# The second norm of a two-block transformer kernel, taken by halves of the tokens

## What is computed

```
x  = x + gate1 * einsum('bsm,md->bsd', mixed, w_out)          # output projection
h2 = rms_norm(x, g_norm2) * (1 + scale2) + shift2             # the second norm
q  = einsum('bsd,dq->bsq', h2, w_q_peer)                      # 2048 query columns
scores = einsum('bshpc,hpnc->bshpn', q, sub_keys)             # then top-k, gather, experts
```

## Time and profile before

| | |
|---|---|
| median of three executions | 3136.06 us (3135.14 to 3137.2) |
| span of the profiled execution, first to last instruction | 3134.2 us |
| PE busy, share of the span | 2990.2 us, 95% |
| DVE busy | 2025.2 us, 65% |
| ACT busy | 1261.6 us, 40% |
| POOL busy | 1157.7 us, 37% |

### The profile page before, as it was taken

How to read it: one execution, slowest core, us unless ns; L and a number is a source line. 1 busy time by engine, 2 the same in 40 slices (tenths; PEclk the granted TensorE clock), 3 DMA queues, 4 the chain that set the end, 5 groups by cost and what they waited for, 6 DMA issues and landing times.

```text
span 3134.2 us, 47541 instructions
## 1 busy us (share of the span) xinstructions
PE 2990.2 (95%) x17673; PEld 2612.4 (83%) x17673; DVE 2025.2 (65%) x3238; ACT 1261.6 (40%) x2075; POOL 1157.7 (37%) x564
## 2 busy tenths in 40 slices
PE   6999999998999999999999999899999998999998
PEld 3766679998988888888887788699999975799986
DVE  4767515999977778788886255466651375466622
ACT  3347333446963333333333334432222446432221
POOL 2420333664014444455553222044444430244442
PEclk9998999999999999999999999799999999999999
DMA  6710223555679999999996211023223420122231
GB/s 247 280 60 1 62 93 96 166 175 191 227 248 350 346 328 341 337 351 350 346 347 229 75 55 41 14 88 94 87 88 101 117 81 1 41 89 93 94 101 67
DMA packets 179876, 509.22 MB, mean 162 GB/s; under 512 B 14881, under 2 KB 72353, under 8 KB 175393
## 3 DMA queue, kind: packets, MB, share of 16 engines
q1 hardware_dynamic: 72288, 262.57, 25.4%
q0 software_dynamic: 37440, 136.40, 11.9%
q10 hardware_dynamic: 70016, 108.54, 10.3%
HBM read 467.60 MB, written 39.85 MB: 162 GB/s over the span
## 4 chain that ended last, share of the span: by engine, by line
PE 87%; ACT 5%; DVE 4%; issue 2%; DMA 1%; ACTq 0%; DVEq 0%
PE ps L1279 23%; PE ps L1230 17%; PE ps L1167 16%; PE ps L1533 8%; PE ps L901 8%; ACT arena L1960 2%; PE ps L1351 2%; PE ps L952 1%; ACT arena L1976 1%; PE ps L1680 1%; PE ps L1299 1%; PE ps L1457 1%; PE ps L1414 1%; PE ps L654 1%; PE ps L1421 1%
## 5 line engine op out<-in xcount | busy, mean ns | idle before, releaser
L2314 POOL TENSOR_TENSOR w_lo<-ring,w_hi 128x1024 fp32r<-128x1024 f32 x300 | 755.0, 2520 | 1387.9 <-ACT w_hi L795 1387.8
L795 ACT ACTIVATE w_hi<-ring 128x1024 fp32r<-128x1024 f32 x500 | 525.4, 1055 | 771.9 <-PE ps L1230 277.4
L1230 PE MATMUL ps<-w_hi,arena_r 128*128 128x512 f32 x1536 | 426.8, 397 | 4.5 <-DVE arena_r L2772 4.5
L1167 PE MATMUL ps<-h_hi,w_hi 128*128 128x384 f32 x1024 | 355.5, 347 | 5.0 <-issue 5.0
L1230 PEld LDWEIGHTS ps<-w_hi,arena_r 128*128 128x128 f32 x1536 | 289.0, 189 | 72.2 <-DVE arena_r L2772 5.0
L1167 PE MATMUL ps<-h_lo,w_hi 128*128 128x384 f32 x1024 | 348.9, 341 | 0.0
L1279 PE MATMUL ps<-h_hi,w_hi 128*128 128x264 f32 (+2 forms) x1536 | 347.5, 298 | 0.6 <-DVE arena L2869 0.5
L1167 PE MATMUL ps<-h_hi,w_lo 128*128 128x384 f32 x1024 | 346.4, 338 | 0.0
L1279 PE MATMUL ps<-h_lo,w_hi 128*128 128x264 f32 (+2 forms) x1536 | 346.2, 297 | 0.0
L1279 PE MATMUL ps<-h_hi,w_lo 128*128 128x264 f32 (+2 forms) x1536 | 345.6, 297 | 0.0
L2327 POOL DMA_INDIRECT arena<-u_rows,arena x128 | 193.4, 1511 | 375.8 <-DVE arena L2748 354.5
(11 more groups left out here) (343 smaller groups left out, 5444.0 us busy)
## 6 DMA issues: line engine op xcount, KB each, us to landing
ring<-weight_stream SPq DMA_DIRECT2D x500, 512.0 KB, 3.7
gates<-arena ACTq DMA_DIRECT2D x12, 2048.0 KB, 7.3
arena<-gates ACTq DMA_DIRECT2D x32, 768.0 KB, 14.3
arena<-w_modulation ACTq DMA_DIRECT2D x17, 1024.0 KB, 5.3
early_acts<-arena ACTq DMA_DIRECT2D x64, 192.0 KB, 2.7
arena<-early_acts ACTq DMA_DIRECT2D x32, 384.0 KB, 7.7
arena<-w_modulation ACTq DMA_DIRECT2D x2, 2560.0 KB, 15.0
x<-x_t ACTq DMA_DIRECT2D x1, 2112.0 KB, 19.5
```

Of the source, the lines that this page charges most:

```text
L795: act.activation(w_hi[:, s, :], ring[:, s, :], ACT.Copy).then_inc(hi_ready, 1)
L1167: last = pe.matmul(ps[:, bank, 0:ND], w, v, start=c == 0 and p == 0, stop=c == DC - 1 and p == 2)
L1230: last = pe.matmul(ps[:, Y_BANKS[b][half], :], a[u], w[v][:, half * BANK:(half + 1) * BANK], start=first and p == 0, stop=final and p == 2)
L2314: pool.tensor_tensor(w_lo[:, s, :], ring[:, s, :], w_hi[:, s, :], ALU.subtract)\
```

## The change

The 512 tokens are taken as two halves of 256 from output tile 4 on.

- PE makes output tiles 0 to 3 whole as before. Then it makes tiles 4 to 7 for the first half of the tokens, and after that the same four for the second half, with the same weights in the four slots. The same holds for the first four query tiles. A half tile is 24 matmuls of 256 columns, so the eight halved tiles have 384 matmuls in place of 192.
- The sums of squares are kept by half, the first half's in bank 4, the second's in bank 5. Squares and sums count 12: chunks 0 to 3 whole (two matmuls of 256 columns), chunks 4 to 7 once for each half. The last two sums of the first half stand inside tile 4 of the second half; the last four of the second half stand inside query tile 0 of the first half.
- ACT takes a root for each half and makes 16 high parts of 256 columns in place of 8 of 512. The transfer of the expert keys, which ACT starts, stands behind the first root. The weight splits for the four query slots stand among the high parts of the first half, since those slots are now free only when output tile 4, 5, 6 or 7 is whole.
- DVE adds tiles 4 to 7 by halves and makes the scaled and the low parts by halves, with the adds of the second half among the splits of the first.
- PE starts the first half of query tile 0 only when all eight chunks of that half are split, no longer chunk by chunk.
- The semaphore for the rows of h is one with that of the scores; nothing is moved by that. One more norm group also shifts which of two buffers some later norms use.

The core of the diff (`half_of` and `half_tokens` are the columns of a half):

```diff
+        Norm.squares += halved
+        Norm.sums += halved
+        Norm.groups += 1 if halved else 0
+        Norm.uses += 1 if halved else 0
...
+        Split.chunks += 2 * chunks if halved else chunks
...
+        n_in2 = Norm([every], SEQ, halved=DC // 2)
...
-            for t in range(2, DC):
+            def square_sum(k):
+                c = k if k < DC else k - DC // 2
+                pe.wait_ge(sq_ready, n_in2.q0 + k + 1)
+                for half in (0, 1) if k < DC // 2 else (k // DC,):
+                    cols = half_of(half)
+                    last = pe.matmul(ps[:, 4 + half, cols], ones, sq1[:, (n_in2.q0 + k) % 2, cols],
+                                     start=c == 0, stop=c == DC - 1)
+                last.then_inc(sq_summed, 1)
+            def half_tile(s, half, between=None):
+                for c in range(DC):
+                    h = h_hi[:, c, half_tokens(half)], h_lo[:, c, half_tokens(half)]
+                    for p, (w, v) in enumerate(three(h, weights(s, c * P, (c + 1) * P))):
+                        last = pe.matmul(ps[:, s, half_of(half)], w, v, start=c == 0 and p == 0, stop=c == DC - 1 and p == 2)
+                    if between is not None:
+                        between(c)
+                return last
+            wait(pe, ln_done, n_in2.g0 - 1)
+            for t in range(2, RING):
                 wait(pe, out_added, t - 3)
-                tile1("w_out", TURN["w_out"] + t // 4, t % 4, t % 4)
-                norm_sums(pe, n_in2, ones, [t - 2])
-            norm_sums(pe, n_in2, ones, [6, 7])
-            pe.wait_ge(out_added, DC)
+                tile1("w_out", TURN["w_out"], t, t)
+                square_sum(t - 2)
+            for half in range(2):
+                for s in range(RING):
+                    if half == 0:
+                        pe.wait_ge(out_added, s + 1)
+                        split_wait(pe, "w_out", TURN["w_out"] + 1, s)
+                        half_tile(s, 0).then_inc(half_made, 1)
+                        square_sum(2 + s)
+                    else:
+                        half_tile(s, 1, lambda c: square_sum(6 + (c == 5)) if s == 0 and c in (3, 5) else None) \
+                            .then_inc(slot_used, 1)
+            for half in range(2):
+                for s in range(RING):
+                    if half == 0:
+                        split_wait(pe, "peer_q", TURN["peer_q"], s)
+                    if s == 0:
+                        pe.wait_ge(out_added, DC + half * RING)
+                        pe.wait_ge(h_split, s_in2.q0 + (half + 1) * DC)
+                    last = half_tile(s, half, lambda c: square_sum(DC + c // 2) if half == 0 and s == 0 and c in (0, 2, 4, 6) else None)
+                    if half:
+                        last.then_inc(slot_used, 1)
             def q_tiles(i):
                 if isinstance(i, int):
-                    first_tiles("peer_q", s_in2, part1)
-                for s in range(2 if isinstance(i, int) else 0, RING):
+                    return
+                for s in range(RING):
                     wait(pe, q_peer_taken, i * RING + (s - 3))
                     tile1("peer_q", TURN["peer_q"] + i, s, s)
             turns(pe, 4, q_tiles)
...
-            def split_and_square(name, n, src, ready):
-                for t in range(DC):
-                    split_next(act, name, t // 4, t % 4)
-                    if t:
-                        norm_square(act, n, src, t - 1, ready)
-                norm_square(act, n, src, DC - 1, ready)
-            split_and_square("w_out", n_in2, lambda c: xf[:, c, :], lambda c: act.wait_ge(out_added, c + 1))
+            def square2(k):
+                c = k if k < DC else k - DC // 2
+                cols = slice(0, SEQ) if k < DC // 2 else half_of(k // DC)
+                wait(act, sq_summed, n_in2.s0 + k - 1)
+                act.wait_ge(out_added, k + 1)
+                act.activation(sq1[:, (n_in2.q0 + k) % 2, cols], xf[:, c, cols], ACT.Square).then_inc(sq_ready, 1)
+            def root2(half):
+                act.wait_ge(sq_summed, n_in2.s0 + DC + RING * half)
+                r = rstd1[:, n_in2.g0 % 2, half_of(half)]
+                act.activation(r, ps[:, 4 + half, half_of(half)], ACT.Ln, bias=col("eps", 0), scale=1.0 / D)\
+                    .then_inc(ln_done, 1)
+                act.wait_ge(ln_done, n_in2.g0 + half + 1)
+                act.activation(r, r, ACT.Exp, scale=-0.5).then_inc(rstd_ready, 1)
+            def high2(half, c):
+                if c < DC - 1:
+                    act.wait_ge(h_raw, s_in2.r0 + half * (DC - 1) + c + 1)
+                else:
+                    act.wait_ge(normed, n_in2.u0 + half + 1)
+                act.activation(h_hi[:, c, half_tokens(half)], h_tmp[:, c % 2, half_of(half)], ACT.Identity,
+                               bias=mod[:, 3 * DC + c:3 * DC + c + 1]).then_inc(h_hi_ready, 1)
+            for t in range(RING):
+                split_next(act, "w_out", 0, t)
+                if t:
+                    square2(t - 1)
+            for k in range(RING - 1, DC):
+                square2(k)
+            root2(0)
             act.dma_start(keys, keys_d).then_inc(later_in, 16)
-            norm_root(act, n_in2, 0, 1.0 / D, 0)
+            for s, chunks in enumerate(((0, 1), (2, 3, 4), (5, 6, 7), ())):
+                split_next(act, "w_out", 1, s)
+                if s == 3:
+                    square2(DC + 2)
+                    square2(DC + 3)
+                for c in chunks:
+                    high2(0, c)
+                if s < 2:
+                    square2(DC + s)
+            root2(1)
             for c in range(DC):
-                high_normed(act, s_in2, c, lambda c: mod[:, 3 * DC + c:3 * DC + c + 1])
+                high2(1, c)
...
-            for t in range(DC):
+            def add_out(t, cols):
+                dve.scalar_tensor_tensor(xf[:, t, cols], ps[:, t % 4, cols], mod[:, 2 * DC + t:2 * DC + t + 1],
+                                         xf[:, t, cols], ALU.mult, ALU.add).then_inc(out_added, 1)
+            def add_second(s):
+                dve.wait_ge(slot_used, used(TURN["w_out"] + 1, s))
+                add_out(RING + s, half_of(1))
+            def scaled2(half, c):
+                if c >= 2:
+                    dve.wait_ge(h_split, s_in2.q0 + half * DC + c - 1)
+                dve.scalar_tensor_tensor(h_tmp[:, c % 2, half_of(half)], xf[:, c, half_of(half)], gains[:, 1, c:c + 1],
+                                         rstd1[:, n_in2.g0 % 2, half_of(half)], ALU.mult, ALU.mult)\
+                    .then_inc(*((h_raw, 1) if c < DC - 1 else (normed, 1)))
+            def low2(half, c):
+                dve.wait_ge(h_hi_ready, s_in2.q0 + half * DC + c + 1)
+                dve.scalar_tensor_tensor(h_lo[:, c, half_tokens(half)], h_tmp[:, c % 2, half_of(half)],
+                                         mod[:, 3 * DC + c:3 * DC + c + 1], h_hi[:, c, half_tokens(half)],
+                                         ALU.add, ALU.subtract).then_inc(h_split, 1)
+            def split2(half, first, end):
+                for c in range(first, end + 1):
+                    if c < end:
+                        scaled2(half, c)
+                    if c > first:
+                        low2(half, c - 1)
+            for t in range(RING):
                 dve.wait_ge(slot_used, used(TURN["w_out"], t))
-                dve.scalar_tensor_tensor(xf[:, t, :], ps[:, t % 4, :], mod[:, 2 * DC + t:2 * DC + t + 1], xf[:, t, :],
-                                         ALU.mult, ALU.add).then_inc(out_added, 1)
+                add_out(t, slice(0, SEQ))
+            for s in range(RING):
+                dve.wait_ge(half_made, s + 1)
+                add_out(RING + s, half_of(0))
             dve.wait_ge(out_added, DC)
             dve.wait_ge(mod_ready, 4)
-            split_normed(dve, s_in2, lambda c: xf[:, c, :], lambda c: gains[:, 1, c:c + 1],
-                         lambda c: mod[:, 3 * DC + c:3 * DC + c + 1])
+            dve.wait_ge(rstd_ready, n_in2.g0 + 1)
+            split2(0, 0, 2)
+            add_second(0)
+            split2(0, 2, 5)
+            add_second(1)
+            split2(0, 5, 8)
+            add_second(2)
+            add_second(3)
+            dve.wait_ge(out_added, DC + RING)
+            dve.wait_ge(rstd_ready, n_in2.g0 + 2)
+            split2(1, 0, 8)
```

More of the change, by code:

```diff
@@ L135, with __init__ @@
     adds = 0
-    def __init__(self, groups, tokens, bank=None, merged=None):
+    def __init__(self, groups, tokens, bank=None, merged=None, halved=0):
         self.chunks = groups
@@ L158, with __init__ @@
     raws = 0
-    def __init__(self, norm=None, chunks=DC):
+    def __init__(self, norm=None, chunks=DC, halved=False):
         self.norm = norm
         self.q0, self.r0 = Split.chunks, Split.raws
-        Split.chunks += chunks
+        Split.chunks += 2 * chunks if halved else chunks
         self.done = Split.chunks
```

(17 more changed lines are left out.)

## The result

The changed kernel takes 3140.01 us (median; 3135.4 to 3145.11 over 16 runs) against 3132.99 for the kernel before in the same comparison (3129.24 to 3140.89 over 16 runs). The ratio of the runs is 1.0015, with a 95% interval of 1.0008 to 1.0022: by it the change makes the kernel slower by 4.7 us, 2.5 to 6.9. The two medians alone lie 7.0 us apart; this text goes by the ratio. The prediction was no change with a small gain, 3134.1; the time lies above its range. Its sign is clear, and it is the wrong one.

A forecast was written before the change was run, and what follows sets the result against it. PE, busy 95% of 3134.2 us, bounds the kernel; 8.1 us lost become 6.1 (pause 2.4, clock 1.6, halving 1.3, starts and drains 0.8). Gain 2.0: span 3132.2, plus 1.9 for the median, 3134.1; range 3130.9 to 3137.5.

The forecast's parts named there:

- Does that cover suffice?: Step on whether 9.3 us of second-half output matmuls hide the first half's norm and split; it left a 2.4 us pause.
- rounds 0, 1 and 2: ACT and DVE work from sum 7 to the first half's last split: 3.3, 4.2 and 4.2 us, together 11.7.
- pause 2.4: Term of the sum: PE's wait ahead of query tile 0, 2.4 us in place of 4.8.
- 2 to 3.6 us, ahead of query tile 0, released by a low part on DVE: Sign to see in the profile after: PE pauses once there, and not between the halves of the query tiles.
- The clock: Term: behind the pause PE's granted clock falls to 0.54 for 3.1 us, costing 1.6 us.
- The rival in which the clock stays up: Rival: no low clock behind PE's pause, so without the 1.6 us: 3132.5 us; chance 0.23.
- Halved matmuls: Term for the output and query tiles: 384 matmuls of 256 columns at 0.119 us each, costing 1.3 us.
- The rival of weight loads: Rival: loads cannot hide behind 256 columns; at 0.17 us a matmul 20 us are lost, 3154; chance 0.02.
- hidden with 0.5 us to spare: Query tiles: second half split 8.4 us after sum 11, against 8.9 us of PE work; its late rival had 0.05.
- The longer chain: Rival: first half's split takes longer, pause 3.6 and clock 2.45 us, 2.1 over forecast: 3136.1; chance 0.20.
- The moved pause: Rival: a 5.01 us pause of PE's instruction issue vanishes or a second appears, 3129 or 3139; chance 0.14.
- Starts, drains and the carry: Terms: 0.8 us of starts and drains, and the first query turn's shift carried one to one to the kernel's end.

The follow-up runs named there:

- e1: Changed kernel, but POOL makes the four query slots' low weights only after DVE has split the whole first half; 3136.49 us, ratio 1.0005 to the kernel before.
- e5: Changed kernel, but ACT makes all eight high parts before the weight splits and DVE makes the query slots' low weights; 3134.18 us, ratio 0.9995 to the kernel before.
- e7: e6 with slot 0's weight split between high parts 3 and 4, second-half adds but one behind the split, last two sums moved; 3130.7 us, ratio 0.9984 to before.
- e6: e5, but query tile 0 of the first half makes its two high-weight products first, the low-weight one last; 3131.86 us, ratio 0.9989 to the kernel before.
- e4: Changed kernel, but POOL makes each query slot's low weights in two instructions of 512 columns instead of one of 1024; 3138.91 us, ratio 1.0014 to the kernel before.

## Why the prediction was wrong

**The failed step: "Does that cover suffice?"** The chain of rounds 0, 1 and 2 was summed from durations taken where POOL did nothing: "scaled and low parts [...] become 0.45 each, 0.47 if waited for". The prediction put the weight splits among the high parts on ACT, costed them as steps of ACT's queue (right: 1.04 to 1.06 each), and used POOL's instruction only for the time at which the weights are ready. It did not ask what POOL's instruction does to DVE beside it. Three low parts took 2.3 us in place of 0.48, the way 17.5 in place of 11.7, and e1 took nearly all of the difference away (12.1) by moving POOL alone. In the sum, the term "pause 2.4" measured 8.45, which is 6.0 us more, and 5.8 of it is the way's.

**The pause "2 to 3.6 us, ahead of query tile 0, released by a low part on DVE"** was right in place and releaser, wrong in size. The text had said that a pause of over 4 us would show it wrong.

**The clock** fell, as forecast, but for 5.60 us where 3.1 was taken: 2.8 us in place of 1.6. For a pause of 2.4 us the step agrees with e5. The extra 1.2 us cannot be put down to the longer pause: behind 3.96 us of pause the kernel before had 0.50 for 5.70 us, more than the changed kernel behind 8.45, so how long the low clock lasts is not in order of the pause and is left open. It also means that segments of single profiles that differ by about 1 us are not told apart by them alone. The rival in which the clock stays up is refuted for this kernel.

**Halved matmuls** were mis-sized a little, to the other side. The output tiles run from 369.98 to 404.50 - 8.45 = 396.05, 26.07 us; less 3.44 of sums that is 22.63 for 192 halved matmuls, where four whole tiles take 22.24. In the query tiles 75 take 8.87, 0.118 each, so 192 take 22.7. Together 0.9 us, not 1.3. The rival of weight loads, which needed 0.124, is refuted.

**Second half "hidden with 0.5 us to spare".** Right, and nearly not: the chain shows 0.06 us of issue at 420.44 between the halves. Sum 11 is done at 411.57, the last low part of the second half ends at 420.36, against PE's 8.87 us of other work: 0.1 us to spare.

**The longer chain** was the rival that came nearest in place, but by the wrong mechanism and at a third of the size (2.1 us over the forecast, where the sum below gives 6.4). Its reason, trips between the engines, does not lengthen the chain: e1 has all of them and takes 12.1.

**The moved pause** was nearest in number (3139), and it did not happen. The pause put down to issue stands where it stood, at 915.50 before and here after:

```profile
916.22 0.66 PE L1216 MATMUL ps<-h_hi,w_hi 128*128 128x384 f32 x1 [5.16 <-issue]
```

It is 5.00 to 5.24 us in all nine profiles, and the next smaller one put down to issue, 2.14 us at 768.76 before, is 2.13 or 2.14 in all nine.

**Starts, drains and the carry "one to one to the end".** 0.35 for 0.8. From 432.1 to the scores the two kernels take 67.5 and 67.5 us, and in all eight rows of the table the difference of the segment lies inside the interval of the ratio. The profiled stretch behind the scores is 1.0 us longer in after than in before; 0.8 of it lies ahead of 915.50 (916.22 after), 0.15 of that in the pause that ends there, and its cause is not known.

**The range.** By its own terms its ends are 3132.5 - 1.3 = 3131.2 and 3137.4; it was written as 3130.9 to 3137.5. Nothing hangs on it.

With 8.45 for 2.4, 2.8 for 1.6, 0.9 for 1.3 and 0.35 for 0.8, the prediction's own sum gives 12.5 in place of 6.1: 6.4 us more than forecast, +4.4 against before.

**What stays open.** In e7 sum 10's square stands on ACT behind the weight splits of slots 1 to 3, which end at 405.71; whether another order of ACT removes the 0.80 us was not tried. Nor was it tried which part of e7's edits is worth what. How much of the whole kernel's time goes to DVE and POOL holding each other up elsewhere was not measured.

## What to carry to other kernels

When a change puts one engine's work beside another's, read what that neighbour does to the durations too: look in the trace for one instruction of the same line and shape with two lengths, and for what ran beside the long one. An instruction that is off the critical path can lengthen one that is on it; here 2.4 us of POOL, three times, cost 5.4 us of chain. And where PE waits for the last of several inputs, its own products can be put in the order in which the inputs come: between e5 and e6 that took 1.3 us from the segment, most of it by keeping the clock up.

## What the runs showed of the hardware

- A DVE instruction with two SBUF tensors as inputs is held while POOL makes low weights in SBUF: 2.31 us in place of 0.48 (after), 2.75 in place of 0.69 (before). With one input in PSUM it takes 0.75 inside POOL's. The Trainium skill states this ("SBUF — State Buffer", section "SBUF: two separate sides"): VectorE and GpSimd share a pair of ports as an exclusive lock, held for a whole instruction, against a VectorE operation with two SBUF inputs. The traces agree.
- The other way round, POOL is held by DVE: the same POOL instruction takes 3.48 us in place of 2.40 when it starts just behind a DVE instruction of 1.22 us (before, 113.84). In these rows the one that starts second is held.
- A held DVE instruction ends 0.28 us after POOL's at 256 columns (after) and 0.56 at 512 (before, 351.49), less than the 0.48 and 0.69 us that it takes alone.
- Cutting POOL's instruction in two frees almost nothing for this chain of DVE parts: 1.23 + 1.38 in e4 for 2.31 + 0.48 in after, and a way of 17.0 for 17.5.
- The same low weights of 1024 columns take DVE 1.22 us and POOL 2.4.
- Matmuls of 256 columns, each with its own weights, start 0.118 us apart over whole tiles, a little over half of the 0.232 of 512 columns.
